# Products of 64 rows on each half of TensorE's array, in the units that are added to x

## The reference

```python
for l in range(DEPTH):
    h = rms_norm(x, mix_norm[l])
    z = h @ w_in[l]
    ...
    x = x + (g_a * y_a + g_b * y_b + g_c * y_c) @ w_mix_out[l]
    h = rms_norm(x, xa_norm[l])
    m = rms_norm(mem, mem_norm[l])
    x = x + cross_attn(h, m, xa_w_q[l], xa_w_kv[l], xa_w_o[l])
    h = rms_norm(x, ffn_norm[l])
    gt, up = jnp.split(h @ ffn_w_in[l], 2, axis=-1)
    x = x + (jax.nn.silu(gt) * up) @ ffn_w_out[l]
return rms_norm(x, final_norm)
```

## Time and profile before

| | |
|---|---|
| median of 3 runs | 2055.92 us (2055.67 to 2056.3) |
| the profiled execution | 2055.54 us, its span 2053.7 us |
| TensorE busy | 2046.0 us, 12515 matmuls |
| VectorE busy | 1197.8 us |
| ScalarE busy | 891.7 us |
| granted TensorE clock, mean | 0.999 of full |

### The profile page before, as it was taken

How to read it: one execution, slowest core, us unless ns; L and a number is a source line. 1 busy time by engine, 2 the same in 40 slices (tenths; PEclk the granted TensorE clock), 3 DMA queues, 4 the chain that set the end, 5 groups by cost and what they waited for, 6 DMA issues and landing times.

```text
span 2053.7 us, 30082 instructions
## 1 busy us (share of the span) xinstructions
PE 2046.0 (100%) x12515; PEld 1694.4 (83%) x12515; DVE 1197.8 (58%) x1832; ACT 891.7 (43%) x1405; POOL 0.4 (0%) x5
## 2 busy tenths in 40 slices
PE   9999999999999999999999999999999999999998
PEld 8888887788888888888888888877888888888887
DVE  6778876665655544443356787766656545444432
ACT  6666544444444323232274665444544433232223
POOL 0000000000000000000000000000000000000000
PEclk9999999999999999999999999999999999999999
DMA  6233232233333333333333323223433323333331
GB/s 187 74 90 90 68 90 76 63 113 114 116 103 97 95 93 102 94 94 95 101 102 87 84 77 79 73 77 88 115 107 112 103 82 103 96 99 98 90 103 59
DMA packets 360975, 194.55 MB, mean 95 GB/s; under 512 B 29724, under 2 KB 350856, under 8 KB 360840
## 3 DMA queue, kind: packets, MB, share of 16 engines
q1 hardware_dynamic: 358872, 189.06, 33.0%
q10 hardware_dynamic: 1968, 3.57, 0.6%
HBM read 189.98 MB, written 2.10 MB: 94 GB/s over the span
## 4 chain that ended last, share of the span: by engine, by line
PE 99%; ACT 0%; DVE 0%; DVEq 0%; issue 0%; POOLq 0%
PE PS L665 27%; PE PS L667 27%; PE PS L666 27%; PE PS L726 4%; PE PS L934 1%; PE PS L984 1%; PE PS L862 1%; PE PS L779 1%; PE PS L780 1%; PE PS L778 1%; PE PS L746 1%; PE PS L748 1%; PE PS L747 1%; PE PS L939 1%; PE PS L963 1%; PE PS L874 0%
## 5 line engine op out<-in xcount | busy, mean ns | idle before, releaser
L1096 ACT ACTIVATE wH<-raw 128x1024 fp32r<-128x1024 f32 (+3 forms) x382 | 375.5, 984 | 840.6 <-PE PS L667 775.4
L665 PE MATMUL PS<-hH,wH 128*128 128x512 f32 x1552 | 608.1, 392 | 0.0
L667 PE MATMUL PS<-hH,wL 128*128 128x512 f32 x1552 | 604.1, 389 | 0.0
L666 PE MATMUL PS<-hL,wH 128*128 128x512 f32 x1552 | 604.1, 389 | 0.0
L1520 DVE TENSOR_TENSOR wL<-raw,wH 128x1024 fp32r<-128x1024 f32 (+2 forms) x380 | 429.6, 1131 | 220.4 <-ACT wH L1096 218.8
L667 PEld LDWEIGHTS PS<-hH,wL 128*128 128x128 f32 x1552 | 291.4, 188 | 61.1
L665 PEld LDWEIGHTS PS<-hH,wH 128*128 128x128 f32 x1552 | 291.4, 188 | 60.6 <-issue 0.9
L666 PEld LDWEIGHTS PS<-hL,wH 128*128 128x128 f32 x1552 | 291.5, 188 | 59.6 <-issue 0.5
L1480 DVE TENSOR_TENSOR gate<-PS,rh 128x512 f32<-128x512 f32 x92 | 63.6, 691 | 148.6 <-PE PS L667 147.1
L665 PE MATMUL PS<-fH,wH 128*128 128x512 f32 x352 | 136.9, 389 | 0.0
L666 PE MATMUL PS<-fL,wH 128*128 128x512 f32 x352 | 136.9, 389 | 0.0
(11 more groups left out here) (365 smaller groups left out, 2964.2 us busy)
## 6 DMA issues: line engine op xcount, KB each, us to landing
raw<-in_w_in SPq DMA_DIRECT2D x106, 512.0 KB, 3.9
raw<-in_ffn_w_in SPq DMA_DIRECT2D x88, 512.0 KB, 3.8
raw<-in_xa_w_kv SPq DMA_DIRECT2D x32, 512.0 KB, 3.8
raw<-in_ffn_w_out SPq DMA_DIRECT2D x32, 512.0 KB, 3.6
raw<-in_w_mix_out SPq DMA_DIRECT2D x16, 512.0 KB, 3.7
raw<-in_xa_w_q SPq DMA_DIRECT2D x16, 512.0 KB, 3.7
raw<-in_xa_w_o SPq DMA_DIRECT2D x16, 512.0 KB, 3.6
raw<-in_ffn_w_out SPq DMA_DIRECT2D x16, 384.0 KB, 3.3
```

What stands on the lines that cost most here:

```text
L665: nc.tensor.matmul(o, w0, xh(k0 + k), start=(first and k == 0), stop=False)
L666: nc.tensor.matmul(o, w0, xl(k0 + k), start=False, stop=False)
L667: ins = nc.tensor.matmul(o, w1, xh(k0 + k), start=False, stop=(last and k == kts - 1))
L1096: nc.scalar.activation(weights_of(n, wH, NS), weights_of(n, raw, NR), ACT.Copy).then_inc(sem("weights_high"), 1)
```

## The change

In the units mix, xo (from unit 2 on) and fo, each matmul of 128 contraction rows becomes two of 64 rows, one on each half of the array's rows. The upper half accumulates in one bank and the lower half in another. `residual()` adds both banks to x, the second after the first has completed. `take_for()` takes the two banks. Weights, activations and their transfers stay as they are.

```diff
+def by_halves(name, j):
+
+    return name in ("mix", "fo") or name == "xo" and j > 1
+
+
+HALVES = (slice(0, P // 2), slice(P // 2, P))
...
                         w0, w1 = wH[:, s, k * m:(k + 1) * m], wL[:, s, k * m:(k + 1) * m]
+                        if by_halves(name, j):
+                            for q, (w, x) in enumerate(((w0, xh(k0 + k)), (w0, xl(k0 + k)), (w1, xh(k0 + k)))):
+                                for o_, r in zip(o, HALVES):
+                                    ins = nc.tensor.matmul(o_, w[r], x[r], start=(first and k == 0 and q == 0), stop=(last and k == kts - 1 and q == 2))
+                            continue
...
+                def take_for(me):
+
+                    if by_halves(*me[1:]):
+                        return [take(l, me, ("half", name, me[2])), take(l, ("rest",) + me[1:], ("ev", name, me[2]))]
+                    return take(l, me, ("ev",) + me[1:])
...
-                    ins = product(take(l, me, ("ev", name, j)), tile(mgH), tile(mgL), key=key)
+                    ins = product(take_for(me), tile(mgH), tile(mgL), key=key)
...
-                    ins = in_two(tile(xoH), tile(xoL), key) if j < 2 else product(take(l, me, ("ev", name, j)), tile(xoH), tile(xoL), key=key)
+                    ins = in_two(tile(xoH), tile(xoL), key) if j < 2 else product(take_for(me), tile(xoH), tile(xoL), key=key)
...
-                        fo_bank[:] = [take(l, ("fo", m_), ("ev", "fo", m_))]
+                        fo_bank[:] = [take_for(("u", "fo", m_))]
...
-                V.tensor_tensor(xT[:, j, :], xT[:, j, :], bank(*step) if name != "fo" else bank("fo", j), ALU.add)\
-                    .then_inc(*did("vector", "ev", name, j))
+                two = by_halves(name, j)
+                V.tensor_tensor(xT[:, j, :], xT[:, j, :], bank("u", name, j), ALU.add).then_inc(*did("vector", "half" if two else "ev", name, j))
+                if two:
+                    dve.wait_ge(*own(l, "vector"))
+                    V.tensor_tensor(xT[:, j, :], xT[:, j, :], bank("rest", name, j), ALU.add).then_inc(*did("vector", "ev", name, j))
```

## The result

The changed kernel takes 2059.18 us (median of 20 runs, 2058.61 to 2059.39); the kernel before takes 2056.37 us (20 runs). The ratio is 1.0013, with a 95% interval of 1.0007 to 1.0019: 2.8 us more, 0.13%. The forecast was 2058.3 us and +2.4 us.

A forecast was written before the change was run, and what follows sets the result against it. TensorE, busy over the whole span, was taken as the bound. 2055.5 us profiled + 0 for pairs + 2.4 for block edges + 0 for second adds gave 2057.9, by the median 2058.3 us; range 2038 to 2082.

The forecast's parts named there:

- The bound, and the price from starts: Whole kernel: TensorE busy over the whole span; a 512-column matmul's price is the distance between starts, 0.2267 us, not 389 ns latency.
- Halves run together: Mix, xo, fo: two 64-row fp32r products take the time of one; rival without concurrency +391.7 us, 2450 us, chance 0.12.
- The price of a pair, 0.2267 us: 1728 touched matmuls: each pair costs what one full product did, so 0 us; ends -18.5 and +23.0 us; chance 0.31.
- the 13 ns: Part of each 512-column matmul's 0.2267 us beyond its 0.2133 us of columns; taken as the same for each concurrent half.
- Both faster rivals: Touched pairs: the 13 ns vanish in 64-row mode (2039.8 us, chance 0.27) or halve with height (2046.8 us, chance 0.12).
- Starts add: Rival, touched pairs: each pair pays 7 ns more between its halves' starts, +12.1 us, 2070.4 us; chance 0.05.
- 13 ns in series: Rival, touched pairs: each half pays its own 13 ns one after the other, +23.0 us, 2081.3 us; chance 0.08.
- Entering and leaving: Edges of the 64-row blocks on TensorE: four gaps of about 0.1 us, 0.4 us a block, six blocks, +2.4 us.
- The second add and the banks: VectorE: 44 extra adds of 0.79 us, 35 us, all covered; two of seven banks a unit, no wait; 0 us.

## Why the prediction was right

- *The bound, and the price from starts.* Right: TensorE is busy 2049.7 of 2057.4 us, and the edges of the blocks account for the whole change.
- *Halves run together.* Right, and it decided most: on one half alone the kernel takes 2450 us. The f32 pairs of the earlier trace rows were a good witness for fp32r.
- *The price of a pair, 0.2267 us.* Right in value, measured over 527 distances and with a lone half. The reason I gave, that no row ties the 13 ns to the rows, was absence of evidence, so that this value came out was partly luck: my own chances had faster at 0.41 and no change at 0.31. The f32 halves, which the argument leaned on, paid 3 ns and not 13. The runs show what the 13 ns go with: 4 new bytes a column in each partition. A half reads as many bytes from each of its partitions as the full product does, and pays the same (0.227 us alone in fp32r), so nothing could be won. Both faster rivals, at 0.39 together, fall with this.
- *Starts add; 13 ns in series.* Both out: 0.227 us a pair. That the packing rule of the Trainium skill ("TensorE: Matmul & The Clock Gate", Part 3) adds about 4 ns for a further tile holds for the distance inside a pair here (the starts lie 3 to 4 ns apart in the changed kernel's trace), not for the distance between pairs.
- *Entering and leaving.* Right place, a little too small: 0.47 us a block measured (2.8 us in 6, 10.6 us in 22) for the 0.4 predicted. The four gaps of 0.1 us were as read; missing was that the next few matmuls settle over another 0.07 us. Six times that is 0.4 us, the whole miss of the sum, 2.4 for 2.8 us.
- *The second add and the banks.* Right: leaving the add out gained nothing. Of TensorE's waits in the changed kernel the list has a single one, on GpSimd at the start, and none on VectorE:

```profile
PE PS L626 <- POOL ones L585: 1.0, 1, 1.0
```

## What to carry to other kernels

Row tiling (products on parts of the array's rows at the same time) didn't make a full-height product cheaper. What it gives is two 64-row products in the time of one (2059 against 2450 us on one half), which helps only where rows would stand empty. Each block of it cost half a microsecond at its edges, so tiled units belong together. Before rearranging a matmul to get rid of a fixed cost, find out what the cost hangs on by changing one operand at a time: three runs that leave out part of the operand settled here what the argument from other shapes had to leave open. When splitting over banks, count how many output tiles' banks are in use at a time: of seven, two for each tile were free, four cost 1.1 us at each of 38 tiles.

## What the runs showed of the hardware

- TensorE starts matmuls of another row group ahead of program order, by about three matmuls: a step with all upper products first took 2058.50 us, as in alternating order, and a unit so ordered 2340.74, where no overlap takes 2450.55. The Trainium skill ("TensorE: Matmul & The Clock Gate", Part 2) says that matmuls stay in program order and only weight loads are pulled ahead; for different row groups these runs differ.
- The fixed part of a 512-column matmul is 13 ns with 4 new bytes a column (fp32r), 12 ns with bf16 elements 4 bytes apart, and some 2.5 ns with 2 new bytes a column or none. Plain f32 at two cycles a column pays 3 ns.
- Going from products of 128 rows to 64-row pairs and back cost 0.47 us together (2.8 us for 6 blocks, 10.6 us for 22).
- 96 weight columns in place of 128 made the same product slower, 0.230 for 0.227 us.
